# Gate and up of half B's first feed-forward layer: seven block products in place of eight

## The reference, cut to what matters

```
def swiglu_ffn(h, w_gate, w_up, w_down):
    return (jax.nn.silu(h @ w_gate) * (h @ w_up)) @ w_down
...
    xp = xp + swiglu_ffn(rms_norm(xp, g_ffn[i]), w_gate[i], w_up[i], w_down[i])
```

## Time and profile before

| | us |
|---|---|
| median of 3 runs | 2187.19 |
| lowest, highest | 2186.01, 2187.87 |
| span of the profiled execution | 2184.5 |
| PE busy in the span | 2163.4 |
| DVE, ACT, POOL busy | 1293.1, 1113.9, 1229.0 |

### The profile page before, as it was taken

The page is one execution under the profiler, slowest core; times in us unless marked ns, Lnnn a source line. Parts: engine busy times, 40 slices in busy tenths (PEclk is TensorE's granted clock), DMA queues, the critical chain, the costliest instruction groups (busy, mean ns, idle before and its releaser), DMA issues.

```text
span 2184.5 us, 35164 instructions
## 1 busy us (share of the span) xinstructions
PE 2163.4 (99%) x13600; PEld 1963.1 (90%) x13600; DVE 1293.1 (59%) x2125; ACT 1113.9 (51%) x1866; POOL 1229.0 (56%) x690
## 2 busy tenths in 40 slices
PE   9899999999999999999999999999999999999999
PEld 8798877888889799999999899888888899999999
DVE  5998787953534545555543545565555248665765
ACT  7556565434424655556552466565665434444443
POOL 3796889975456443333334654433343456768775
PEclk9999999999999999999999999999999999999999
DMA  5112323332333522222222342222222223333232
GB/s 156 49 49 59 89 89 97 97 95 89 96 97 93 116 79 78 86 71 76 80 80 83 97 103 78 88 86 79 86 81 84 83 92 109 96 116 98 83 112 81
DMA packets 313651, 194.19 MB, mean 89 GB/s; under 512 B 40374, under 2 KB 286734, under 8 KB 313486
## 3 DMA queue, kind: packets, MB, share of 16 engines
q1 hardware_dynamic: 311608, 190.83, 29.5%
q10 hardware_dynamic: 1878, 1.11, 0.2%
HBM read 184.39 MB, written 5.10 MB: 87 GB/s over the span
## 4 chain that ended last, share of the span: by engine, by line
PE 87%; DVE 8%; POOL 2%; issue 1%; ACT 1%; DMA 0%; SPq 0%; DVEq 0%; POOLq 0%; ACTq 0%
PE ps L491 48%; PE ps L751 11%; PE ps L833 10%; PE ps L758 5%; DVE ps L1910 4%; PE ps L862 4%; PE ps L870 2%; PE ps L722 1%; PE ps L707 1%; PE ps L525 1%; DVE hBl L1807 1%; PE ps L683 1%; PE ps L682 1%; POOL accp L2489 1%; DVE hB L1801 1%
## 5 line engine op out<-in xcount | busy, mean ns | idle before, releaser
L2458 POOL TENSOR_TENSOR wlo<-raw,whi 128x1024 fp32r<-128x1024 f32 x280 | 694.9, 2482 | 800.7 <-PE ps L491 500.3
L1169 ACT ACTIVATE whi<-raw 128x1024 fp32r<-128x1024 f32 x280 | 295.9, 1057 | 376.7 <-PE ps L491 203.4
L491 PE MATMUL ps<-hAh,whi 128*128 128x512 f32 x1056 | 410.1, 392 | 2.2 <-ACT hAh L1220 0.9
L491 PE MATMUL ps<-hAl,whi 128*128 128x512 f32 x1056 | 408.0, 390 | 0.2
L2005 DVE TENSOR_TENSOR x<-ps,x 128x512 f32<-128x512 f32 (+1 forms) x368 | 259.5, 706 | 205.8 <-PE ps L758 124.5
L491 PE MATMUL ps<-hBh,whi 128*128 128x272 f32 x1472 | 301.1, 289 | 6.0 <-DVE gxA L1869 3.6
L491 PE MATMUL ps<-hBl,whi 128*128 128x272 f32 x1472 | 302.4, 290 | 0.8
L491 PE MATMUL ps<-hAh,wlo 128*128 128x512 f32 x1056 | 267.9, 396 | 0.0
L491 PEld LDWEIGHTS ps<-hAh,whi 128*128 128x128 f32 x1056 | 198.0, 188 | 45.9 <-ACT hAh L1209 1.7
L491 PEld LDWEIGHTS ps<-hBh,whi 128*128 128x128 f32 x1472 | 229.7, 189 | 8.6 <-issue 4.1
L491 PEld LDWEIGHTS ps<-hAl,whi 128*128 128x128 f32 x1056 | 198.3, 188 | 41.8 <-DVE hAl L1807 1.2
(11 more groups left out here) (331 smaller groups left out, 4373.6 us busy)
## 6 DMA issues: line engine op xcount, KB each, us to landing
raw<-in_w_gate_dram SPq DMA_DIRECT2D x78, 512.0 KB, 3.7
raw<-in_w_up_dram SPq DMA_DIRECT2D x78, 512.0 KB, 3.8
raw<-in_w_down_dram SPq DMA_DIRECT2D x76, 512.0 KB, 3.5
raw<-in_w_pw_dram SPq DMA_DIRECT2D x38, 512.0 KB, 4.0
raw<-in_w_qkv_dram SPq DMA_DIRECT2D x32, 256.0 KB, 3.6
raw<-in_w_o_dram SPq DMA_DIRECT2D x64, 128.0 KB, 2.9
wraw<-in_w_down_dram SPq DMA_DIRECT2D x12, 512.0 KB, 4.4
wraw<-in_w_gate_dram SPq DMA_DIRECT2D x10, 512.0 KB, 5.2
```

What stands on the lines that cost most here:

```text
L491: ins = nc.tensor.matmul(o, wt[n % 2][:, P * k:P * (k + 1)], src[h][:, k, c0:c0 + w], start=start, stop=stop)
L1169: nc.scalar.activation(whi[n % 2][:], raw[n % 2][:], ACT.Copy).then_inc(w_hi, 1)
L2458: nc.gpsimd.tensor_tensor(wlo[n % 2][:], raw[n % 2][:], f(whi[n % 2][:]), ALU.subtract).then_inc(w_lo, 1)
```

## The change

The gate and up tiles of `G` = 1 to 10 in `ffn(0, "B")` go over to the seven-product scheme; `G` = 0 stays with `proj`, and `down` keeps its matmuls. `ffn_v` takes the place of `ffn(0, "B")` on every engine.

- PE: `v_products` for gate and for up, each 7 products of 4 blocks x 3 passes = 12 matmuls, 84 in all, where two `proj` had 96. 240 matmuls of 272 columns fall away in the program (8238 before, 7998 now). The attention hangs at products 1, 4, 8 and 11 of the 14 (`V_TURN`).
- Weights: two `raw` buffers only. Sum S3 is written over block A21 in `raw`; `vs1`, `vs2`, `vs4` hold the others. A buffer is loaded anew when POOL has split the blocks out of it and DVE has made all four sums.
- ACT and POOL: a tile of 1024 becomes two blocks of 512, and a pair has seven instead of eight halves' worth of two tiles: 18 blocks of 512 for each `G`, where there were 6 tiles of 1024. ACT copies two of the seven results out of PSUM.
- DVE, for each `G`: 8 weight sums of 512 columns, 16 additions of 272 columns; `times_up` and `act_low` stay two each.
- DVE, once: two activation sums in `qkv("A")` (`v_first_terms`), and in `G` = 0 five additions of 1088 columns, four low parts and four weight sums, between the q work. `act_low` of `G` = 0 moves to `G` = 1.
- Memory: `x` is cut into `xA` and `xB`; `xA` (2 MB) is written to DRAM during `qkv("A")` and read back behind the last weight load of the stage, both on SP's queue. Its room holds `t1h`, `t1f`, `t1l`, `t2h`, `vs1`. The loads of the caches on ACT's queue move behind the stage.

```
+        V_TURN = (1, 4, 8, 11)
+        VWIN = ["A11", "A12", "S3", "A22", "S2", "S1", "S4"]
...
+            def v_products(w, G):
+
+                j, att = v_pair(G, w), "A"
+                for i in range(7):
...
+                    take(key, "A")
+                    if j == 0 and 2 <= i <= 4:
+                        pe.wait_ge(r_lo, i)
...
+                    pe.wait_ge(v_hi, m + 1)
+                    for k in range(4):
+                        product(whi, rh, k, start=(k == 0))
+                        ins = product(whi, rl, k)
+                    ins.then_inc(v_read, 1)
+                    at = 7 * (w == "U") + i
+                    if at in V_TURN:
+                        b = V_TURN.index(at)
+                        if G >= 2:
+                            turn(att, G - 2, b)
+                        if (G, b) == (1, 0):
+                            drain((4, 5, 6, 7))
+                        scores(att, G - 1, b)
+                    pe.wait_ge(v_lo, m + 1)
+                    for k in range(4):
+                        ins = product(wlo, rh, k, stop=(k == 3))
+                    ins.then_inc(pfull[place[key][0]], 1)
+                    if at - 1 in V_TURN and G >= 2:
+                        values(att, G - 2, V_TURN.index(at - 1))
...
+                    if r < 4:
+                        j = 2 * g + r // 2
+                        sp.wait_ge(v_lo, v_start(j) + (4 if r % 2 else 2))
+                        sp.wait_ge(v_sum, 4 * j + 4)
...
+                full(sp, ("V", "U", NG - 1, 5))
+                sp.dma_start(x["A"][:], x_spill.rearrange("p (k n) -> p k n", k=KD)).then_inc(x_back, 16)
...
+                if h == "A":
+                    sp.wait_ge(xn_ready, KD * 3)
+                    sp.dma_start(x_spill.rearrange("p (k n) -> p k n", k=KD), x["A"][:]).then_inc(x_out, 16)
...
+            def v_sum_up(w, G, i):
...
+                if i == 4:
+                    plus(vc["c12"], bank(key[4]), vc["c12"]).then_inc(fr(key[4]), 1)
+                    freed(dve, key[3])
+                    freed(dve, key[4])
+                    plus(vc["c22"], vc["c22"], vc["c12"]).then_inc(v_acc, 1)
+                    plus(vc["c21"], vc["c21"], vc["c12"]).then_inc(v_acc, 1)
...
+                for G in range(1, NG):
+                    cur, prev = G - 1, G - 2
+                    j = v_pair(G, "G")
+                    v_act_low(G - 1, 0)
+                    turned_low(att, prev, 0)
+                    v_sum_up("G", G, 1)
+                    linked()
+                    read_scores(att, cur, 0)
+                    v_act_low(G - 1, 1)
+                    v_sum_up("G", G, 3)
+                    out_sum(att, prev, 0)
+                    v_weight_sum(j + 1, "S1")
+                    v_weight_sum(j + 1, "S3")
+                    turned_low(att, prev, 1)
+                    v_sum_up("G", G, 4)
+                    out_low(att, prev, 0)
+                    v_sum_up("G", G, 5)
+                    read_scores(att, cur, 1)
...
```

More of the change, by code:

```diff
@@ L177, in build @@
             ckv = sb("ckv", [P, 2, 2 * P], F32, c)
+        with ExitStack() as c:
+            vs4 = sb("vs4", [P, 512], F32, c)
         qsh = sb("qsh", [P, 2, 4 * TS], F32R)
@@ L197, in build @@
             qraw = [sb(f"qraw{s}", [P, N["B"]], F32, c) for s in range(KD)]
+        with ExitStack() as c:
+            t3f = sb("t3f", [P, 4, CWB], F32, c)
+            t4f = sb("t4f", [P, 4, CWB], F32, c)
+            t4h = sb("t4h", [P, 4, CWB], F32R, c)
+            t4l = sb("t4l", [P, 4, CWB], F32R, c)
         act_hl = [sb(f"act{s}{w}", [P, N["B"]], F32R) for s in range(4) for w in "hl"]
```

495 lines of the change are left out of this document (476 added, 19 removed).

## The result

The changed kernel takes **2211.05 us** (median of 4 runs, 2209.62 to 2217.35), the kernel before 2186.80 (2186.01 to 2187.87): the ratio is 1.0117, 95% interval 1.0105 to 1.013. The forecast was 2171, with a range up to 2186. The change is slower by 24 us where 16 us less were forecast.

The account below looks back on a forecast made before the run. The prediction took PE to bound the kernel, busy 2163.4 of 2184.5 us. Matmuls -30.0, passage +8, full `G` waits +5 and transfers +1 gave -16.0, so 2187.2 became 2171 us, range 2160 to 2186.

Parts of the forecast that it names:

- The matmuls removed: On PE, 240 matmuls at 0.125 us fall away, -30.0 us; a full `G` goes from 41.20 to 38.20 us.
- It fits, with 2.9 us to spare: In a full `G`, DVE's pass takes 35.3 of 38.2 us, or 92%, on an in-order queue.
- 22 pieces at 0.27 us of delay: DVE instructions of a `G` that read SBUF twice or are blocked so; 0.27 us is the mean sum's delay beside POOL.
- The term of +5 us: Small PE waits for DVE, 0.7 us in each of seven full `G` (2 to 8); bounds 0 and 14 us.
- DVE is the bound: Rival: in the full `G`, DVE's 35.3 us plus hand-over waits make 40.2, not 38.9; 2180 us, chance 0.22.
- the lock on shared reads: Rival: DVE pieces each wait half a POOL block, 0.65 us, for a pass of 43.7 us; 2205 us, chance 0.07.
- point of decision: In the lock rival, the DVE pass of 41.2 us from which the stage's gain is gone but for three `G`.
- The passage, +8 us: From `G` = 0 to 1, PE waits for DVE's queued low parts and score read; bounds 3 and 12 us.
- ACT, POOL and the loads at nothing: In a full `G`, ACT at most 31.8 and POOL 25.4 of 38.2 us, weight loads in time; no cost.
- the transfers at +1: `xA`'s 2 MB spill and read-back on SP's queue stay mostly hidden; +1 us, bounds 0 and 3.
- over 40.5 us: Sign that the prediction is wrong: a full `G` longer than this, where 38.5 to 39.5 us was expected.
- passage above 12: Sign that the prediction is wrong: the passage from `G` = 0 to `G` = 1 costing more than 12 us.

Follow-up runs that it names:

- e1: Changed kernel with POOL's low parts of the stage's weight blocks made for only 16 of 512 columns; 2164.78 us.
- e14: Changed kernel with POOL's low parts made for 16 of 512 columns in `G` = 2 to 8 alone; 2184.13 us.
- e13: e11 with sums S1 and S3 put back to their earlier place and ACT making `turned_high(2)` earlier; 2174.05 us.
- e11: Changed kernel with POOL in halves, bank sums with PSUM, DVE's passage, V and down part reordered, sink copies on ACT; 2183.67 us.
- e15: Changed kernel with POOL's low parts made for 16 of 512 columns in `G` = 1 alone; 2202.40 us.

## Why the prediction was wrong

- **The matmuls removed, -30 us: right.** With the lock gone a full `G` takes 38.3 us; 38.20 was forecast.
- **"It fits, with 2.9 us to spare": the step that failed.** DVE's pass was put at 35.3 us, and its busy time is 37.0, only 1.7 more. Taken apart, 22 pieces at 0.27 us of delay are 5.9 of the 35.3, so its free part was 29.4 (e1 and e14 show 28.9 and 29.1); the lock costs 8.1 us, or 0.37 us for each of the 22. The error lay in what was set beside it: DVE is idle another 5.2 us in each `G`, waiting mostly for ACT's halves of the attention and for PE, and the hand-overs kept the queue from filling this time. 37.0 + 5.2 = 42.2 is the beat. The term of +5 us (0.7 for each `G`) measured 28.1 over the 267.4 that matmuls need, also past its bound of 14. In all the kernels above with POOL at work the `G` is 5 to 9 us longer than DVE's busy time; a pass of 35 was no room under 38.2. How much of the 5.2 us is the order of the queue stays open: the mended hand-over took the `G` from 40.4 to 39.0 with POOL in halves (e13 against e11), and no run has that order with POOL's whole instructions.
- **The rivals.** "DVE is the bound" had the mechanism and 40.2 us; "the lock on shared reads" had it with its cause, and 2205. It had a chance of 0.07. Its price of 0.65 us a piece was too high and its point of decision, a pass of 41.2 us busy, too late: at 37.0 it was slower. The argument held against it, that POOL is less busy here than where the 941 ns were measured, is refuted: POOL's share was 60% against 75%, and the weight sums took 1176 ns in the mean (65.8 us for 56 in the table of DVE's groups with its other two forms). The share of POOL's time doesn't tell how often a sum meets the start of a POOL instruction.
- **The passage, +8 us: the place right (DVE's queue), the size too small and the wait of product 2 put on the wrong instruction.** It measured 18.4 (848.94 against 830.6), of which e15 takes 9.7 away. The wait for product 2 was 3.2 us where 5.0 were forecast, and ended with the second product with up and not with the low part of `t3f`; the score reads cost 2.5 where 1.1 was. Missed was the wait of 2.97 us in the last projection of `G` = 0, for the bank that the first product with up frees; that instruction stood in DVE's queue behind three activation sums, a low part and four pieces of the q work, and the walk began at the norm at 780 and looked at PE from product 2 on only. The four waits are 8.7 us together; most of the rest is the lowered clock.
- **The end of the stage, forecast at nothing: 13.8 us.** No `G` after the eighth was walked through. PE waits 1.4, 1.8 and 1.8 us in `G` = 9, all for DVE, and the granted clock falls behind the last two. With a thin POOL everywhere `G` = 9 takes 36.7 us (e1), here 47.2.
- **The clock** was in no term. In this execution it adds some 12 us (an estimate, above), behind waits for DVE. With POOL thin in `G` = 1 it stays at 1.00 there.
- **ACT, POOL and the loads at nothing, the transfers at +1: right.** PE waits for no weight in the full `G`, and the q projections show no gap: the stage begins at 770.60 and began at 770.61. The spill was issued at 699.12 and had landed at 708.05, 8.9 us later, near the 9.1 us that the prediction takes without showing their working. Its other value, 6.8 us, was too short. It comes from a fit that the Trainium skill (DMA: Bandwidth & Descriptors, Anatomy of one DMA — SWDGE (gpsimd) path) gives for transfers that GpSimd issues; this one is issued by SP.
- Of the marks named ahead, "over 40.5 us" and "passage above 12" both came, and the third (PE waiting for weights) did not, which is what pointed at DVE.
